# Squared-relu stages of a two-block kernel: seven block products of half the tokens in place of eight in the second product of parts 1 to 3, two of the weight sums on GpSimd

## What is computed

```python
D_FF_2 = 4 * D_MODEL                       # 4096
h2 = rms_norm_2(x, norm2) * (1.0 + scale2) + shift2
ff = jnp.square(jax.nn.relu(h2 @ w_ff1)) @ w_ff2
return x + gate2 * ff
```

## Time and profile before

| | |
|---|---|
| runs | 3095.34, 3094.89, 3094.22 us |
| median | 3094.89 us |
| span of the profiled execution, first to last instruction | 3089.4 us |
| busy: PE, PEld, DVE, ACT, POOL | 99%, 80%, 54%, 36%, 22% |
| DMA | 329.70 MB, mean 107 GB/s |

### The profile page before, as it was taken

How to read it: one execution, slowest core, us unless ns; L and a number is a source line. 1 busy time by engine, 2 the same in 40 slices (tenths; PEclk the granted TensorE clock), 3 DMA queues, 4 the chain that set the end, 5 groups by cost and what they waited for, 6 DMA issues and landing times.

```text
span 3089.4 us, 36733 instructions
## 1 busy us (share of the span) xinstructions
PE 3055.2 (99%) x14530; PEld 2474.7 (80%) x14530; DVE 1675.0 (54%) x2491; ACT 1109.0 (36%) x1757; POOL 678.0 (22%) x525
## 2 busy tenths in 40 slices
PE   9999999999999999999999999999999999999999
PEld 7888887788888888887788888777788877778887
DVE  6454557654555445527864555687533356763332
ACT  4222344432223232234443222456422233643331
POOL 2101134111011110054211101256211123721110
PEclk9999999999999999999999999999999999999999
DMA  5344422343443434431143444301333331033332
GB/s 191 116 154 127 133 85 72 93 134 121 157 128 121 126 121 157 128 105 62 34 137 116 133 137 137 107 29 55 102 96 97 98 104 61 17 108 103 96 95 75
DMA packets 115802, 329.70 MB, mean 107 GB/s; under 512 B 13616, under 2 KB 19120, under 8 KB 115248
## 3 DMA queue, kind: packets, MB, share of 16 engines
q1 hardware_dynamic: 115632, 327.36, 33.8%
HBM read 325.21 MB, written 2.10 MB: 106 GB/s over the span
## 4 chain that ended last, share of the span: by engine, by line
PE 92%; DVE 3%; ACT 2%; POOL 1%; issue 1%; DMA 0%; SPq 0%; DVEq 0%; ACTq 0%; POOLq 0%
PE ps L79 91%; PE ps L82 1%; POOL s_tmp L96 1%; ACT s_tmp L85 1%; DVE s_tmp L88 1%; DVE s_wl L88 1%; DVE s_tmp L108 0%; ACT s_wh L85 0%; DVE s_small L102 0%; ACT s_hh L85 0%; DVE s_x L91 0%; POOL s_tmp L88 0%; DVE s_tmpr L88 0%; DVE s_hl L88 0%; DMA s_raw<-in_f1i_dram 0%
## 5 line engine op out<-in xcount | busy, mean ns | idle before, releaser
L85 ACT ACTIVATE s_wh<-s_raw 128x1024 fp32r<-128x1024 f32 (+3 forms) x560 | 541.9, 970 | 1109.0 <-PE ps L79 1107.9
L79 PE MATMUL ps<-s_hh,s_wh 128*128 128x512 f32 x2304 | 895.2, 394 | 18.6 <-ACT s_hh L85 11.6
L88 DVE TENSOR_TENSOR s_wl<-s_raw,s_wh 128x1024 fp32r<-128x1024 f32 (+3 forms) x529 | 609.4, 1153 | 531.9 <-ACT s_wh L85 531.3
L79 PE MATMUL ps<-s_hh,s_wl 128*128 128x512 f32 x2304 | 887.8, 390 | 0.2
L79 PE MATMUL ps<-s_hl,s_wh 128*128 128x512 f32 x2304 | 886.7, 390 | 0.3 <-DVE s_hl L88 0.3
L88 POOL TENSOR_TENSOR s_tmp<-s_tmp 128x512 f32<-128x512 f32 (+2 forms) x228 | 315.5, 1388 | 1615.1 <-ACT s_tmp L85 1454.0
L79 PEld LDWEIGHTS ps<-s_hh,s_wh 128*128 128x128 f32 x2304 | 433.9, 189 | 115.6 <-issue 16.8
L79 PEld LDWEIGHTS ps<-s_hh,s_wl 128*128 128x128 f32 x2304 | 433.9, 188 | 92.6 <-DVE s_wl L88 2.1
L79 PEld LDWEIGHTS ps<-s_hl,s_wh 128*128 128x128 f32 x2304 | 433.6, 188 | 92.0 <-issue 2.2
L79 PE MATMUL ps<-s_a0h,s_wh 128*128 128x512 f32 x960 | 377.3, 393 | 0.0
L79 PE MATMUL ps<-s_a0h,s_wl 128*128 128x512 f32 x960 | 373.8, 389 | 0.0
(11 more groups left out here) (141 smaller groups left out, 2992.4 us busy)
## 6 DMA issues: line engine op xcount, KB each, us to landing
s_raw<-in_ff_dram SPq DMA_DIRECT2D x128, 512.0 KB, 3.7
s_tmp<-in_w_mod_dram SPq DMA_DIRECT2D x192, 256.0 KB, 3.6
s_raw<-in_f1i_dram SPq DMA_DIRECT2D x88, 512.0 KB, 3.7
s_raw<-in_f2i_dram SPq DMA_DIRECT2D x88, 512.0 KB, 3.6
s_raw<-in_f1o_dram SPq DMA_DIRECT2D x32, 512.0 KB, 3.6
s_raw<-in_f2o_dram SPq DMA_DIRECT2D x32, 512.0 KB, 3.6
s_raw<-in_hyb_dram SPq DMA_DIRECT2D x28, 512.0 KB, 3.6
s_raw<-in_nsa_dram SPq DMA_DIRECT2D x28, 512.0 KB, 3.6
```

The costliest lines, as they stand in the source:

```text
L79: return self.eng.matmul(o, w, m, **kw) if self.eng is not None else Blank()
L85: return self.eng.activation(o, a, f, **kw) if self.eng is not None else Blank()
L88: return self.eng.tensor_tensor(o, a, b, f) if self.eng is not None else Blank()
```

## The change

The second product of parts 1 to 3 is done by groups, one for a pair of output tiles d, d+1. A group takes a 2 x 2 block form: the weights of the two units in blocks of (512 hidden features) x (one output tile), the hidden activations in blocks of (512 features) x (half the tokens: SOONER 0 to 255, LATER 256 to 511). Eight products of such blocks become seven (Winograd's form): three of them take sums of weight blocks, three take sums of activation blocks (`a1h`, `a1l` now hold these). Each is 4 k-tiles x 3 matmuls of 128x256.

- Weight sums: GpSimd makes the first (`first_sum`) and the third (`third_sum`, written over the low half of `wl`'s slot as `wlf`), VectorE the second and fourth; ScalarE makes the high and VectorE the low parts of all four. They are double buffered in `tmp` slots 38 to 40 and 41 to 43 (44 to 49).
- Activation sums: after the second evac of a pair (hidden tiles t and t+4, hence the order `UP_TILE`), VectorE makes four differences of 256 columns, ScalarE two high parts, VectorE two low parts.
- Outputs: two of the four banks of a group are added to x as before (one over 256 columns), two are kept in SBUF (`keep`, `PAIRS`), added up over the three parts, and added into x by `sum_up` in part 4's up units.
- The order is up 1, first unit of up 2, groups of part 1, rest of up 2, first unit of up 3, groups of part 2, and so on. Part 4's down units stay as they were, with k-tiles in the order `UP_TILE`. Slots of relu are four in place of three. The raw slot of a group's first unit comes free with `low_dif` of its second.

The core of the diff:

```diff
+UP_TILE = (0, 4, 1, 5, 2, 6, 3, 7)
+UP_BANK = ((0, 1, 2, 3, 4, 5, 6, 3), (7, 0, 1, 2, 3, 4, 5, 6))
+LATER, SOONER = slice(T // 2, T), slice(0, T // 2)
...
+            def block(b, half, w_h, w_l, hi, lo, mov):
+                for k in range(4):
+                    mh, ml, sig_h, key_h, sig_l, key_l = mov(k)
+                    w = slice(k * 128, (k + 1) * 128)
+                    pe.wait_ge(*hi)
+                    pe.wait_ge(*sig_h[key_h])
+                    pe.matmul(ps[:, b, half], w_h[:, w], mh, start=k == 0, stop=False)
+                    pe.wait_ge(*sig_l[key_l])
+                    pe.matmul(ps[:, b, half], w_h[:, w], ml, start=False, stop=False)
+                    pe.wait_ge(*lo)
+                    m = pe.matmul(ps[:, b, half], w_l[:, w], mh, start=False, stop=k == 3)
+                return m
...
+                claim(b0)
+                block(b0, LATER, wh[:, c0, 0:T], wl[:, c0, 0:T], w_hi[u0], w_lo[u0], a_part(0, LATER))
+                block(b0, SOONER, Sr(sum_hi(u1, 0)), Sr(sum_lo(u1, 0)), g_hi[u1, 0], g_lo[u1, 0], t_part(0)).then_inc(
+                    *g_mm.up((u0, 0)))
+                free[b0] = [(x_add, (s, p, d, "51"))]
+                claim(b1)
+                block(b1, SOONER, Sr(sum_hi(u1, 1)), Sr(sum_lo(u1, 1)), g_hi[u1, 0], g_lo[u1, 0], t_part(1))
+                block(b1, LATER, wh[:, c1, 0:T], wl[:, c1, 0:T], g_hi[u1, 2], g_lo[u1, 2], t_part(2)).then_inc(
+                    *g_mm.up((u0, 1)))
+                free[b1] = [(x_add, (s, p, d, "67"))]
+                claim(b2)
+                block(b2, LATER, wh[:, c0, T:2 * T], wl[:, c0, T:2 * T], w_hi[u0], w_lo[u0], a_part(4, LATER)).then_inc(
+                    *unit.up(u0))
+                block(b2, SOONER, Sr(sum_hi(u1, 2)), Sr(sum_lo(u1, 2)), g_hi[u1, 1], g_lo[u1, 1], a_part(4, SOONER)).then_inc(
+                    *g_mm.up((u0, 2)))
+                free[b2] = [(x_add, (s, p, d))]
+                claim(b3)
+                block(b3, LATER, wh[:, c1, T:2 * T], wl[:, c1, T:2 * T], w_hi[u1], w_lo[u1], t_part(3)).then_inc(
+                    *unit.up(u1))
...
+            def group(s, p, d, u0, l):            # VectorE, n = u0 + 3
+                if n in stream.second:
+                    low_last(n)
+                    second_sum(n)
+                    fourth_sum(n)
+                else:
+                    weights(n)
+                dve.wait_ge(*g_mm[u0, 0])
+                keep(r0, b0, (s, p, d, "51"))
+                if n in stream.second:
+                    low_sums(n)
+                    low_dif(n)
+                dve.wait_ge(*g_mm[u0, 1])
+                keep(r1, b1, (s, p, d, "67"))
+                if n in stream.second:
+                    low_fourth(n)
+                dve.wait_ge(*g_mm[u0, 2])
+                dve.scalar_tensor_tensor(x[:, d, :], B(b2), mod[:, l, 5, d:d + 1], x[:, d, :], ALU.mult, ALU.add)
+                weights(u0 + 4)
+                dve.wait_ge(*unit[u1])
+                dve.scalar_tensor_tensor(x[:, d + 1, LATER], ps[:, b3, LATER], mod[:, l, 5, d + 1:d + 2], x[:, d + 1, LATER],
+                                         ALU.mult, ALU.add).then_inc(*x_add.up((s, p, d + 1)))
...
+                        if i % 2 and p < 3:           # VectorE, evac of the second tile of a pair
+                            dve.wait_ge(*prod[s, p, i])
+                            dve.tensor_tensor(t12[:, SOONER], first[:, SOONER], first[:, LATER], ALU.subtract)
+                            dve.tensor_tensor(t34[:, SOONER], last[:, SOONER], first[:, SOONER], ALU.subtract)
+                            dve.tensor_tensor(t12[:, LATER], last[:, SOONER], t12[:, SOONER], ALU.subtract)
+                            dve.tensor_tensor(t34[:, LATER], last[:, LATER], t12[:, LATER], ALU.subtract)
...
+                    if kind == "sums":                # GpSimd
+                        first_sum(step[1])
+                    elif kind == "load":
+                        third_sum(step[1])
+                    elif kind == "group":
+                        first_sum(step[3] + 3)
+                        third_sum(step[3] + 3)
```

More of the change, by code:

```diff
@@ L137, in add, with group @@
         return len(self.src) - 1
+    def group(self, us):
+        self.first.add(us[0])
+        self.second.add(us[1])
 def plan_ffn(stream, win, wout, late_norm=False):
@@ L449, in plan_rel @@
 def plan_rel(stream, w1, w2):
[L450 to L474, removed]
+    order = []
+    def up(p, ts):
+        for i in ts:
+            order.append((("up", p, i), [stream.add(w1[8 * p + UP_TILE[i]], 1024)]))
+    def down(p):
+        for d in range(0, KT, 2):
+            us = [stream.add(w2[d + m, :, p * 1024:(p + 1) * 1024], 1024) for m in range(2)]
+            if p == 3:
+                order.extend((("down", p, d + m), [us[m]]) for m in range(2))
+            else:
+                stream.group(us)
+                order.append((("group", p, d), us))
@@ new lines, in plan_rel @@
+    four = [stream.add(w1[UP_TILE[i]], 1024) for i in range(4)]
+    up(0, range(4, 8))
+    up(1, range(1))
+    down(0)
+    for p in (1, 2, 3):
+        up(p, range(1, 8))
+        if p < 3:
+            up(p + 1, range(1))
+        down(p)
+    steps = [("mean",), ("scale", 0), ("load", four[3])] + [("scale", d) for d in range(1, KT)] + [("first", four)]
+    for i in range(3):
+        steps.extend([("load", four[3] + 1 + i), ("evac", 0, i)])
+    before, added = (0, 3), None
+    for what, us in order:
+        kind, p, i = what
+        if kind == "up":
+            steps.append(("up", p, i, us[0]))
+        elif kind == "down":
+            steps.append(("down", p, i, us[0]))
+        else:
+            steps.append(("group", p, i, us[0]))
+            if p == 2 and i == KT - 2:
+                steps.extend([("sum", 4), ("sum", 6)])
+        if added:
+            steps.append(("add",) + added)
+        if kind != "group":
+            n = us[0] + AHEAD
+            if n not in stream.second:
+                steps.append(("load", n))
@@ L477, in down @@
                 before = None
[L478 to L492, removed]
+            if n in stream.second:
+                steps.append(("load", n))
+            if n + 1 in stream.second and n - 1 not in stream.second:
+                steps.append(("sums", n + 1))
+            if (kind, p) == ("up", 3) and i in (3, 5):
+                steps.append(("sum", i - 3))
+        if added:
+            steps.append(("tile", added[1]))
+            added = None
+        if kind == "up":
+            before = (p, i)
+        elif kind == "down":
+            added = (p, i)
+    return steps + [("add",) + added, ("tile", added[1])]
 def two_block_kernel(nc, ins, out):
@@ L1770, in weights @@
                 c = u % RING
+                if u in stream.second:
+                    low_last(u)
+                    low_dif(u)
+                    return
                 dve.wait_ge(*w_hi[u])
@@ L2333, in rel @@
                         weights(step[1])
+                    elif kind == "sums":
+                        second_sum(step[1])
+                        fourth_sum(step[1])
+                        low_sums(step[1])
+                        low_fourth(step[1])
                     elif kind == "scale":
@@ L2341, in rel @@
                     elif kind == "add":
                         _, p, d = step
-                        add(s, p, d, unit_at[s, "down", p, d], mod[:, l, 5, d:d + 1], p == 3)
+                        dve.wait_ge(*x_add[s, "sum", d])
+                        add(s, p, d, unit_at[s, "down", p, d], mod[:, l, 5, d:d + 1], True)
+                    elif kind == "sum":
+                        sum_up(s, step[1], l)
+                    elif kind == "group":
+                        _, p, d, u0 = step
+                        group(s, p, d, u0, l)
```

222 lines of the change are left out of this document (198 added, 24 removed).

## The result

The changed kernel takes 3117.39 us (median of 4 runs, 3113.01 to 3119.95) against 3094.55 us before: ratio 1.0077, 95% interval 1.0064 to 1.0089. 22.8 us were lost, where a gain of 29.5 us was forecast. The profiled execution has a span of 3111.2 us against 3089.4.

What follows compares the result with a forecast made beforehand. TensorE's matmuls were taken to bound the kernel. Narrower matmuls gain 31.2 us, less 1.5 at the turns and 0.2 in the last parts: 29.5 us, so 3065.4 us; own range 3059 to 3072, wider range 3058 to 3083.

Steps and rivals of the forecast that it cites:

- What bounds the kernel: Whole span: TensorE's matmuls bound it (busy 99%); matmul time saved comes off the span, other engines' added work is free within gaps.
- The price c of a 256-column step: Groups: a 256-column matmul with its weight load steps at 0.114 us, so 2016 replace 1152 wider ones, gaining 31.2 us.
- rival (a): Group matmuls: 13 ns are paid at every weight change, step 0.120 us, gain 19.1 - 1.7, 3077.5 us; chance 0.13.
- the two equations: Stick-breaking score products, 64-row pairs: L + 2s = 0.34 for 256 columns, L + 4s = 0.57 for 512, giving s = 0.115.
- L: Stick-breaking score products: the one weight load that nothing hides between the first and last pair, taken as 0.11 us.
- The weight load hides behind 256 columns: Group matmuls: a 128x128 weight load of 0.111 us just fits behind a 256-column stream of 0.113 us.
- rival (c): Group matmuls: the weight load does not hide; at 0.188 us per step, 118 us more than before, 3213 us; chance 0.04.
- The cover at the turns: Turn from up units to groups: one up unit (5.4 us) put between nearly hides the operand preparation; 0.25 us each, 1.5 us.
- The collision of GpSimd and VectorE: Groups and turns: each GpSimd weight sum slows VectorE by up to 0.5 us; inside groups booked at zero.
- rival (b): Groups: VectorE becomes the bound, held for each GpSimd sum's whole 1.29 us; only 10 us gained, 3085 us; chance 0.12.
- From span to time: Whole kernel: the median run stands 5.5 us above the profiled span (start and end), so span 3059.9 becomes 3065.4 us.
- What the change adds elsewhere: Up units, sum_up, raw slot waits: nothing reaches TensorE; the last part's down unit waits 0.1 us, twice.

Runs made afterwards that it cites:

- the cut one: Kernel before the change, its down units of parts 1 to 3 issued as 256+256, 4 x 128 and 384+128 columns, without groups: 3202.91 us (one run).

## Why the prediction was wrong

**What bounds the kernel**: right. What was on TensorE's path came off or onto the span, and the rest stayed within its 2825 to 2832 us.

**The price c of a 256-column step**: the term of 31.2 us was mis-sized. It is 0.1200, not 0.114, in the changed kernel and in the cut one; the gain of the columns is 19.1 us. That is rival (a), which I gave 0.13 and against which I held. Those rows can't exclude it: a fixed part stands in both widths, so it cancels in the difference of the two equations and ends up in L. And they are one stretch of several. An earlier stretch of 64-row matmuls in the trace of the kernel before has these second and third pairs of 256 columns (a row can merge two pairs; what counts is its start):

```profile
454.67 0.41 PE L79 MATMUL ps<-s_tmpr 64*128 64x256 f32 x4
454.79 0.29 PE L79 MATMUL ps<-s_tmpr 64*128 64x256 f32 x2
```

Their step is 0.121 us by the single starts (454.667 and 454.788); in the stretch of the earlier trace rows it is 0.118. Of the steps from a second to a third pair of this width in that trace, 18 are 0.121 or 0.122 and 9 are 0.117 to 0.119. So the nearest shape already had about the 0.120 of the full one. The other estimate, half of 0.2266, assumed what was to be shown. The 0.2266 itself, 0.0133 above 512 columns at 2.4 GHz, spoke as much for the value at the end of my range as for the one I took.

**The weight load hides behind 256 columns**: right, rival (c) is out: load-bound steps are 0.1116 us.

**The cover at the turns**, booked at 1.5 us in six turns and costing 44: this is the step that failed and turned the sign. I walked ScalarE's queue from the cover unit on and put it 0.25 us late. Two things stand before that point. The step "sums" of the first group lies in front of the relu of (p, 6) and waits for VectorE, which puts the relu of (p, 7) 3.3 us later than forecast; moving that step one unit up brings back 19 us by itself. And at a stage's first turn the evacs are 10 us behind from the four units at the start; I took the steady stretch for all six turns, and the first turns cost more than twice the others (12 us over 40.3 against 5).

**The collision of GpSimd and VectorE**, at up to 0.5 us each: four differences take 1.55 us alone, 2.63 beside one GpSimd sum, 3.70 beside two, so 1.05 to 1.1 us for a sum of 1.29. Two such sums and the late relu together bring the low part at the second turn at 11.7 us after the cover unit's first matmul, where it was due at 8. I misread: several GpSimd instructions are merged in that row, and the one in VectorE's way is short (the same trace, at the start of VectorE's),

```profile
1955.32 0.72 POOL L88 TENSOR_TENSOR s_tmp<-s_tmp 128x256 f32<-128x256 f32 x1
```

and starts 0.07 us before VectorE's. VectorE's 1.20 for 0.69 was 0.5 us lost to an instruction of 0.72, not a bound for one of 1.29. The Trainium skill, SBUF — State Buffer, section SBUF: two separate sides, says that who comes second blocks fully; for VectorE behind GpSimd the trace comes near to it. For GpSimd behind VectorE the trace shows both: the square takes 1.59 for 1.29 with 0.7 us of overlap, so it loses less than half of it, but in the steady groups of the changed kernel the third sum takes 2.08, with 0.93 us of overlap with the subtraction before it, and loses 0.79:

```profile
2236.22 0.75 DVE L94 SCALAR_TENSOR_TENSOR s_x<-ps,s_mod,s_x 128x512 f32<-128x512 f32 x1 [1.59 <-PE ps L82]
2236.89 1.81 DVE L91 TENSOR_TENSOR s_wl<-s_raw,s_wh 128x1024 fp32r<-128x1024 f32 x1
...
2236.33 1.29 POOL L91 TENSOR_TENSOR s_tmp<-s_raw 128x512 f32<-128x512 f32 x1 [10.88 <-PE ps L82]
2237.77 2.08 POOL L91 TENSOR_TENSOR s_wlf<-s_raw 128x512 f32<-128x512 f32 x1
```

**Waits inside the groups**, rival (b): did not come. VectorE's lead of one group was enough: in the second and third parts TensorE runs 336 matmuls without a wait once the turn is mended, with VectorE busy 33 of 40 us, and with 10 us of GpSimd beside it.

**The clock** was in no step of the forecast, though it takes 12.8 of the 44 us. In the changed kernel each wait of 3 us at a turn is followed by steps at 1.2 GHz, which cost 1.6 us; in the first turns the waits are 7.6 us in sum, and the granted clock over the part is 0.87. Where the waits are gone (40.31 us parts) it is 1.00.

**From span to time**: the prediction puts the 5.5 us between the median and the profiled span down to the start and the end. In every profiled execution with a recorded time the two lie 1.8 to 1.9 us apart (3113.01 against 3111.2); the rest fits the spread of the runs of that kernel, 3091.11 to 3095.34. The forecast is the same without it, 29.5 us off the median.

**What the change adds elsewhere** (sum_up, the raw slots, the last part's down units): nothing, as forecast. The eight down units of part 4 take 43.6 us.

## What to carry to other kernels

When a product is cut into narrower ones, price the step of the narrow matmul by a run of just that shape, not by an equation in which a fixed part cancels: with a fixed 13 ns beside 107, a saving of one eighth in columns was 7% in time. A step that moves work ahead costs nothing only if the whole queue of every engine it goes through is read from the last point where that engine had slack; a wait of one engine for another in front of the critical evac is a loss that no busy share shows. And a new stall of some microseconds on TensorE is to be counted with the clock that may fall behind it, here half as much again.

## What the runs showed of the hardware

- A 128-row fp32r matmul with its own weight load steps at its columns / 2.4 GHz + 13 ns: 0.1200, 0.1737, 0.2267 us for 256, 384, 512. At 128 columns it steps at 0.1116, as the loads of the earlier trace rows do.
- Two 64-row matmuls side by side step at 0.117 to 0.122 us for 256 columns, most of them at 0.121 or 0.122, and mostly at 0.235 for 512 (kernel before).
- A GpSimd sum of 128x512 (1.29 us) stretches VectorE's two-input work on SBUF by 1.05 to 1.1 us at the turns; a VectorE add that reads PSUM keeps its 0.75 us with such a sum beside it for 0.64 us. A sum that starts behind a VectorE subtraction took 2.08 us.
- The clock behind waits: in the changed kernel 27.4 us of waiting in six turns brought 12.8 us more at 1.2 GHz; with GpSimd's sums held, waits of 1.9 us brought it in two turns and not in a third, and waits of 0.6 us and less never did at a second or third turn (0.6 with all sums on VectorE, 0.3 with the early sums).
